# Delta rule and attention of a hybrid transformer layer: the strict mask first and its row factor on VectorE, turned k and q earlier, high parts on ScalarE and GpSimd, other places for early tiles

## The chip, the cores and the metric

One core of one Trainium2 chip runs the whole layer in one launch. The metric is the device time of that launch in microseconds. A core has TensorE (PE in the rows; PEld is its weight load), VectorE (DVE), ScalarE (ACT), GpSimd (POOL) and SyncE (SP, which here only issues DMAs). The engines run their own queues in order and meet only at semaphores.

## What is computed

One layer on 2048 tokens of width 1024, float32. Cut to what matters here:

```python
qkv = silu(causal_dwconv(q, k, v)); q, k = l2_norm(q), l2_norm(k)      # 4 heads of 128
g = cumsum(log decay) in each chunk of 64; decay = exp(g_i - g_j) for j <= i
lower = where(j < i, (beta_i k_i . k_j) * decay, 0)      # strict: the mask "below"
attn  = where(j <= i, (q_i . k_j) * decay, 0)            # inclusive: the mask "upto"
u, w  = solve(I + lower, [v * beta, k * beta * exp(g)])
# scan over chunks: v_new = u - w S;  o = q exp(g) S + attn v_new;  S = exp(g_last) S + k_dec^T v_new
o_gdn = rms_norm(o) * silu(z)
o_mla = block-causal softmax attention, 4 heads, keys of 128 + 64 rotary columns
x = layer_norm(ALPHA x + [o_gdn, o_mla] w_out); then a SwiGLU feed-forward, a second norm,
x + sigmoid(x w_ple_gate) * (p w_ple)
```

## The kernel before

The program runs eight stages one behind the other, with a barrier of all engines between them: in-projection (tile names begin with in_), latents (lat_), delta rule (dr_), attention (at_), output projection (op_), feed-forward in (ff_), feed-forward out (fd_) and the gated embedding (em_). Outside the delta rule, products are made from split operands: a float32 is cut into a high part in fp32r and a low part (value minus high part), and three matmuls (hi*lo, lo*hi, hi*hi) stand for one.

**Delta rule** (`delta_rule`). 16 tiles of 128 tokens (two chunks), all four heads at a time as [128, 4, 128]. The order is written out by hand. `steps()` gives 19 rounds; in round r tile m=r is begun ("first"), tile e=r-1 has its 16x16 diagonal blocks inverted ("base"), tile n=r-2 is solved ("solve"), and tile t=r-3 advances the state ("advance"). Each engine has its own list of calls per round, in order:

- TensorE: `a_ws(t,0)`, `s_z(n,0)`, `a_out(t-1)`, `a_kv(t,0)`, `p_turn(m)` (transposes k into b1 and q into b0, L1096), `a_ws(t,1)` (L1180), `a_o(t,0)`, `s_y(n,0)`, `a_kv(t,1)`, `p_turn_v(m)`, `s_z(n,1)`, `a_o(t,1)`, `s_y(n,1)`, `p_gram_k(m)` (k.k into b0, L1132), `s_wu(n)`, `p_gram_q(m)` (q.k into b3, L1138, which raises `gram_done`).
- VectorE: `a_v(t,0)` (L1471), `s_z(n,0)`, `a_s(t,0)` (the state, four scalar_tensor_tensor, L1480), `a_v(t,1)`, `a_gate`, `s_u(n,0)`, `a_s(t,1)`, `p_kdec`, `p_newton`, `p_factors` (makes `made`, among it L's row factor), `p_kbg`, `s_z(n,1)`, `s_u(n,1)`, `p_lower(m)` (L = b0 * dec[:, 0], L1434), `p_attention(m)` (L1439), `spread(e)` (L1449), `a_norm(t)`.
- GpSimd: `sums(m)` (L1031), `substitute(e)` (29 small operations, L1039, L1047, L1049), `decayed(m)` (qdT, L1064), `masks(m)`: decay times `upto` (L1054), decay times `below` (L1056), and that times L's row factor (L1059).
- SyncE stores L to DRAM once `L_done` is raised, waits for the store, and reads the diagonal blocks of it back as `blk` for `substitute`.

`p_turn(m)` waits for `L_done` of the tile before (b0 must have been read). `spread(e)` gives `U`, for which `s_z(n,0)` of the next round waits.

**Attention** (`attention`). 32 blocks (4 heads, 8 query blocks of 256 rows in the order 7,0,6,1,5,2,4,3), 144 steps of one pair of key tiles each. Per step TensorE turns the probabilities of two steps ahead (L1702), multiplies values (L1716 to L1718) and makes score groups three blocks ahead (L1685 to L1689); VectorE makes the low part of the turned probabilities (`low`, L1814) and the maxima (L1782); ScalarE makes their high part (L1751) and the exponentials (L1738); GpSimd scales a block's probabilities (L1651). In steps 2 to 21 of each of the first three heads the next head's operands are split, 16 pieces of 128x512 read through a ring of 4 `raw` buffers: kind 0 is q, 1 is k, 2 is the rotary part of q (two copies), 3 is v. The high part is copied by VectorE (`split_highs`, L1825, L1826, L1828), the low part is made by GpSimd (L1659, L1662), and SyncE loads a buffer again once the low part of its last piece is done. Even heads use the tiles that stand in `at.parts` (made by `AttentionEarly`), odd heads tiles of the stage's own. TensorE waits for `const_sem` (the identity, made by GpSimd) before its first score.

**Places.** Most tiles are placed by an allocator, upwards. The classes derived from `Early` place theirs, counted down from the top of the usable SBUF, so that they can be loaded in the stage before: the even heads' operands, `kr` and `kr_hi`; `op_w_raw`, `ff_x_raw`, `ff_w_raw`; the split weights `fd_w_hi`, `fd_w_lo`, `em_w_hi`, `em_w_lo`. `top` is 229368 rounded down to a multiple of 32: 229344, which is 96 past a multiple of 128. So all of these begin 96 bytes past a multiple of 128.

## Time and profile before

| | us |
|---|---|
| median of 3 runs (lowest, highest) | 3357.72 (3351.21, 3359.09) |
| the profiled execution | 3339.58 |
| its span | 3338.0 |
| TensorE busy | 3081.1 (92%) |
| VectorE, ScalarE, GpSimd busy | 1648.7, 1056.6, 1057.2 |

The profiled execution is 18 us below the median of the others. By the names in the trace, the delta rule takes the time from about 663 to 1058 us, attention from 1061 to 1460, the output projection to 1669, feed-forward in to 2560, feed-forward out from 2568 to 3086, the embedding from 3096 to 3328. TensorE is the busy engine in all of them; where it is idle or at half clock, another engine or a DMA was waited for. A row's duration of a matmul is a modelled one that overlaps the next; counts in a stretch tell its pace.

### The profile page before, as it was taken

Reading aid. Unit: us, or ns where it says so; the run is one execution under the profiler, and the core shown is the slowest. Engines: PE = TensorE matmul, PEld = TensorE weight load, DVE = VectorE, ACT = ScalarE, POOL = GpSimd, SP = SyncE. Lnnn points to the kernel's source line nnn. Section 1 sums busy time; section 2 is a strip of 40 time slices with the busy share of each in tenths; the row PEclk is TensorE's granted clock in tenths of the full one; section 3 lists DMA queues with packets and bytes.
Section 4 is the critical chain, followed back from the end, with each engine's and each line's share of the span. In section 5 each row is a group of like instructions: output and inputs, shape, how many; then the busy total and the mean of one; then the engine's idle time right before and its main releaser. Section 6 shows DMA issues by size and latency. Waiting matters only on the chain. (4 is left out here: it accounts for less than half of the span.)

```text
span 3338.0 us, 44243 instructions
## 1 busy us (share of the span) xinstructions
PE 3081.1 (92%) x15074; PEld 2541.3 (76%) x15074; DVE 1648.7 (49%) x2773; ACT 1056.6 (32%) x2363; POOL 1057.2 (32%) x1184
## 2 busy tenths in 40 slices
PE   7999997869997889989979999899998999999898
PEld 5888885658886777878758888788887788887776
DVE  3654004536665777656585555865555433233433
ACT  2111014335554444542243333433333211111321
POOL 2322241066665555410073333543331000000122
PEclk9999998979998989999989999999999999999999
DMA  3211115422324211125723222232223433233433
GB/s 137 87 75 75 75 57 183 143 75 75 82 63 106 61 50 54 67 76 181 239 69 115 94 75 80 71 117 94 76 79 111 136 97 96 90 96 122 148 121 99
DMA packets 284412, 329.17 MB, mean 99 GB/s; under 512 B 33280, under 2 KB 224640, under 8 KB 279936
## 3 DMA queue, kind: packets, MB, share of 16 engines
q1 hardware_dynamic: 238632, 265.84, 25.0%
q0 software_dynamic: 12384, 45.09, 3.8%
q10 hardware_dynamic: 33280, 16.78, 1.8%
q8 instruction: 62, 1.02, 0.1%
q14 instruction: 54, 0.44, 0.0%
HBM read 210.73 MB, written 116.92 MB: 98 GB/s over the span
## 5 line engine op out<-in xcount | busy, mean ns | idle before, releaser
L2061 PE MATMUL ff_bank<-ff_x_hi,ff_w_lo 128*128 128x512 f32 x1240 | 488.3, 394 | 32.8 <-DVE ff_w_lo L2241 22.0
L2062 PE MATMUL ff_bank<-ff_x_lo,ff_w_hi 128*128 128x512 f32 x1240 | 487.4, 393 | 0.0
L2063 PE MATMUL ff_bank<-ff_x_hi,ff_w_hi 128*128 128x512 f32 x1240 | 486.9, 393 | 0.0
L2044 POOL TENSOR_TENSOR ff_w_sum<-ff_w_raw 128x512 f32<-128x512 f32 x210 | 299.6, 1436 | 496.9 <-DVE ff_w_lo L2241 438.0
L2061 PEld LDWEIGHTS ff_bank<-ff_x_hi,ff_w_lo 128*128 128x128 f32 x1240 | 235.7, 190 | 85.2 <-DVE ff_w_lo L2241 25.0
L296 PE MATMUL in_h_ps<-in_x_hi,in_w_lo 128*128 128x512 f32 x704 | 276.6, 393 | 25.0 <-POOL in_w_lo L252 25.0
L2451 PE MATMUL fd_acc<-fd_w_hi,fd_a_lo 128*128 128x512 f32 x704 | 280.1, 398 | 10.8 <-DVE fd_a_lo L2435 10.7
L2452 PE MATMUL fd_acc<-fd_w_lo,fd_a_hi 128*128 128x512 f32 x704 | 278.3, 395 | 0.0
L2453 PE MATMUL fd_acc<-fd_w_hi,fd_a_hi 128*128 128x512 f32 x704 | 278.1, 395 | 0.0
L297 PE MATMUL in_h_ps<-in_x_lo,in_w_hi 128*128 128x512 f32 x704 | 276.1, 392 | 0.0
L298 PE MATMUL in_h_ps<-in_x_hi,in_w_hi 128*128 128x512 f32 x704 | 276.0, 392 | 0.0
L2063 PEld LDWEIGHTS ff_bank<-ff_x_hi,ff_w_hi 128*128 128x128 f32 x1240 | 235.8, 190 | 49.7
L2062 PEld LDWEIGHTS ff_bank<-ff_x_lo,ff_w_hi 128*128 128x128 f32 x1240 | 235.8, 190 | 49.0
L2140 ACT ACTIVATE ff_w_hi<-ff_w_sum 128x512 fp32r<-128x512 f32 x210 | 132.5, 631 | 288.3 <-PE ff_bank L2063 267.1
L2435 DVE TENSOR_TENSOR fd_a_lo<-fd_a_raw,fd_a_hi 128x256 fp32r<-128x256 f32 x176 | 74.5, 423 | 286.2 <-ACT fd_a_hi L2425 286.2
L2425 ACT ACTIVATE fd_a_hi<-fd_a_raw 128x256 fp32r<-128x256 f32 x176 | 73.4, 417 | 361.4 <-PE fd_acc L2453 356.5
L1651 POOL TENSOR_TENSOR at_prob<-at_prob,at_scale 128x1536 f32<-128x1536 f32 (+4 forms) x112 | 137.8, 1261 | 149.3 <-DVE at_scale L1808 141.1
L296 PEld LDWEIGHTS in_h_ps<-in_x_hi,in_w_lo 128*128 128x128 f32 x704 | 133.4, 189 | 53.8 <-issue 16.8
L2530 POOL DMA_DIRECT2D scratch_x<-fd_w_raw x16 | 8.5, 534 | 511.8 <-DVE fd_w_raw L2631 511.8
L2451 PEld LDWEIGHTS fd_acc<-fd_w_hi,fd_a_lo 128*128 128x128 f32 x704 | 132.2, 188 | 45.1 <-DVE fd_w_lo L2432 10.8
L2453 PEld LDWEIGHTS fd_acc<-fd_w_hi,fd_a_hi 128*128 128x128 f32 x704 | 132.2, 188 | 32.7
L2452 PEld LDWEIGHTS fd_acc<-fd_w_lo,fd_a_hi 128*128 128x128 f32 x704 | 132.3, 188 | 31.4
(380 smaller groups left out, 6582.6 us busy)
## 6 DMA issues: line engine op xcount, KB each, us to landing
ff_w_raw<-w_gate_up SPq DMA_DIRECT2D x44, 1024.0 KB, 5.1
scratch_hT<-in_out SPq DMA_DIRECT2D x22, 1024.0 KB, 3.9
fd_a_raw<-scratch_hid SPq DMA_DIRECT2D x176, 128.0 KB, 2.1
dr_qkv<-scratch_hT SPq DMA_DIRECT2D x16, 768.0 KB, 5.1
in_w_raw<-w_in POOLq DMA_DIRECT2D x22, 512.0 KB, 3.9
scratch_hid<-ff_first SPq DMA_DIRECT2D x44, 256.0 KB, 2.3
scratch_hid<-ff_second SPq DMA_DIRECT2D x44, 256.0 KB, 2.3
fd_w_raw<-w_down SPq DMA_DIRECT2D x22, 512.0 KB, 5.3
```

What stands on the lines that cost most here:

```text
L296: pe.matmul(acc, w_lo[:, b, ws], x_hi[:, k, ts], start=(k == 0), stop=False)
L297: pe.matmul(acc, w_hi[:, b, ws], x_lo[:, k, ts], start=False, stop=False)
L298: last = pe.matmul(acc, w_hi[:, b, ws], x_hi[:, k, ts], start=False, stop=(k == KD - 1))
L1651: last = pool.tensor_tensor(view, view, by, ALU.mult)
L2044: pool.tensor_tensor(w_sum[:, SUM_SLOT[m]], w_raw[:, b, one], w_raw[:, b, two], op).then_inc(w_sum_done, 1)
L2061: pe.matmul(acc, w_lo[:, wm, ws], x_hi[:, xm, k], start=first_mm, stop=False, skip_group_check=skip)
L2062: pe.matmul(acc, w_hi[:, wm, ws], x_lo[:, xm, k], start=False, stop=False, skip_group_check=skip)
L2063: return pe.matmul(acc, w_hi[:, wm, ws], x_hi[:, xm, k], start=False, stop=last_mm, skip_group_check=skip)
L2140: act.activation(w_hi[:, m], src, ACT.Copy).then_inc(w_hi_done, 1)
L2451: pe.matmul(to, self.a_lo[:, slot, rows], self.w_hi[:, k, cols], start=(k == k0), stop=False)
L2452: pe.matmul(to, self.a_hi[:, slot, rows], self.w_lo[:, k, cols], start=False, stop=False)
L2453: last = pe.matmul(to, self.a_hi[:, slot, rows], self.w_hi[:, k, cols], start=False, stop=(k == k1))
```

## The change

Six things, in three parts of the program.

In the delta rule: (1) GpSimd runs `masks(m)` ahead of `decayed(m)`, with `below` first, then `upto`; the third operation (row factor, L1059) is gone, so `masked` counts 2 a tile. (2) VectorE's `p_lower` applies the row factor: four scalar_tensor_tensor, one a head, in place of one tensor_tensor; it waits for the first mask alone, and `p_attention` for the second. (3) TensorE runs `p_turn(m)` straight after `a_ws(t, 0)`.

In attention: (4) VectorE's `split_highs` is gone. ScalarE copies the high parts of q and of the rotary part, and GpSimd makes those of k and v by adding a zero that is broadcast from a [128, 1] tile, ahead of the low part. (5) TensorE waits for the identity at its first transpose and no longer before its first score.

Places: (6) `top` is rounded down to a multiple of 128 (229248), so that every early tile begins at a multiple of 128. Of the tiles that TensorE reads with them: `fd_a_hi` and `fd_a_lo` begin 32 past a multiple of 128 before and now, `em_a_hi`, `em_a_lo` and the odd heads' operands at 0. The new `zero` tile moves those placed after it in attention by 32 bytes: `prob` from 0 to 32, `pT_hi` and `pT_lo` from 64 to 96.

```diff
@@ class Early
-        top = self.nc.sbuf_usable_end // 32 * 32
+        top = self.nc.sbuf_usable_end // P * P
@@ delta_rule, GpSimd
             def masks(m):
                 pool.wait_ge(dec_done, m + 1)
+                reached(pool, L_done, m)
+                pool.tensor_tensor(dec[:, 0], dif[:, m % 2], each(below[:]), ALU.mult).then_inc(masked, 1)
                 reached(pool, attn_done, m)
                 pool.tensor_tensor(dec[:, 1], dif[:, m % 2], each(upto[:]), ALU.mult).then_inc(masked, 1)
-                reached(pool, L_done, m)
-                pool.tensor_tensor(dec[:, 0], dif[:, m % 2], each(below[:]), ALU.mult).then_inc(masked, 1)
-                pool.wait_ge(masked, 3 * m + 2)
-                pool.wait_ge(made_done, 3 * (m + 1))
-                pool.tensor_tensor(dec[:, 0], dec[:, 0], heads(made[:, m % 2, 2]), ALU.mult).then_inc(masked, 1)
...
                 if m is not None:
+                    masks(m)
                     decayed(m)
-                    masks(m)
@@ delta_rule, TensorE
                 if advance:
                     a_ws(t, 0)
+                if first:
+                    p_turn(m)
                 if solve:
                     s_z(n, 0)
...
                     a_kv(t, 0)
-                if first:
-                    p_turn(m)
@@ delta_rule, VectorE
-                reached(dve, masked, 3 * (m - 1))
...
             def p_lower(m):
                 dve.wait_ge(gram_done, m + 1)
-                dve.wait_ge(masked, 3 * m + 3)
+                dve.wait_ge(masked, 2 * m + 1)
...
-                dve.tensor_tensor(L[:, m % 3], b0[:], dec[:, 0], ALU.mult).then_inc(L_done, 1)
+                for h in range(HEADS):
+                    op = dve.scalar_tensor_tensor(L[:, m % 3, h], b0[:, h], made[:, m % 2, 2, h:h + 1], dec[:, 0, h],
+                                                  ALU.mult, ALU.mult)
+                op.then_inc(L_done, 1)
...
             def p_attention(m):
                 dve.wait_ge(gram_done, m + 1)
+                dve.wait_ge(masked, 2 * m + 2)
@@ attention, GpSimd
             def low(h, m):
-                pool.wait_ge(split_high, count + 1)
+                if kind % 2 == 0:
+                    pool.wait_ge(act_high, count // 2 + 1)
+                else:
+                    if h > 1 and m == 1:
+                        pool.wait_ge(pv_done, pair0[NB * (h - 1)])
+                    pool.wait_ge(raw_loaded[slot], sum(32 if j % 4 == 2 else 16 for j in range(slot, count + 1, RAW)))
+                    high = (k_hi if kind == 1 else v_hi)[b]
+                    pool.tensor_tensor(high[:, ts], src, zero[:, 0:1].broadcast_to([P, NTOK]), ALU.add).then_inc(pool_high, 1)
+                    pool.wait_ge(pool_high, count // 2 + 1)
...
+            pool.memset(zero[:], 0.0).then_inc(const_sem, 1)
@@ attention, TensorE
             def turn(n, p):
+                if k == 0:
+                    pe.wait_ge(const_sem, 3)
...
-            pe.wait_ge(const_sem, 2)
@@ attention, ScalarE
+            def split_high(h, m):
+                count, slot, kind, ts = piece(h, m)
+                b, src = h % 2, raw[:, slot]
+                if h > 1 and m == 0:
+                    act.wait_ge(pv_done, pair0[NB * (h - 1)])
+                act.wait_ge(raw_loaded[slot], sum(32 if j % 4 == 2 else 16 for j in range(slot, count + 1, RAW)))
+                if kind == 2:
+                    reached(act, split_low, count + 1 - 4)
+                    act.activation(qr_hi[:], src, ACT.Copy)
+                    act.activation(qr[b][ROPE:, ts], src[ROPE:], ACT.Copy).then_inc(act_high, 1)
+                else:
+                    act.activation(q_hi[b][:, ts], src, ACT.Copy).then_inc(act_high, 1)
...
                 for group in now:
                     exps(*group)
+                for h, m in pieces:
+                    if m % 2 == 0:
+                        split_high(h, m)
@@ attention, VectorE
-                for h, m in pieces:
-                    split_highs(h, m)
```

How the rows of two queues stand. GpSimd in a round of the delta rule, from the end of a substitution (`dr_inv`) to the start of the next; before:

```order
L1049 TENSOR_TENSOR dr_inv<-dr_inv,dr_part 32x14
L1064 TENSOR_TENSOR dr_qdT<-dr_qkv,dr_eg 128x512
L1054 TENSOR_TENSOR dr_dec<-dr_dif,dr_upto 128x512
L1056 TENSOR_TENSOR dr_dec<-dr_dif,dr_below 128x512
L1059 TENSOR_TENSOR dr_dec<-dr_dec,dr_made 128x512
L1031 TENSOR_TENSOR dr_cums<-dr_upto,dr_scal 128x512
L1039 TENSOR_TENSOR dr_inv<-dr_ident_b,dr_blk 32x256
```

and of the change:

```order
L1049 TENSOR_TENSOR dr_inv<-dr_inv,dr_part 32x14
L1054 TENSOR_TENSOR dr_dec<-dr_dif,dr_below 128x512
L1056 TENSOR_TENSOR dr_dec<-dr_dif,dr_upto 128x512
L1061 TENSOR_TENSOR dr_qdT<-dr_qkv,dr_eg 128x512
L1031 TENSOR_TENSOR dr_cums<-dr_upto,dr_scal 128x512
L1039 TENSOR_TENSOR dr_inv<-dr_ident_b,dr_blk 32x256
```

Between the substitution and what `p_lower` waits for stood four operations; now there is one.

TensorE from one round's last product (q.k) to the next round's `a_ws(t, 1)`; before:

```order
L1138 MATMUL dr_b<-dr_qkv 128x128 x4
L1180 MATMUL dr_b<-dr_S,dr_wT 64x128 x4
L1151 MATMUL dr_b<-dr_ident,dr_U 128x128 x2
L1153 MATMUL dr_b<-dr_U,dr_L 128x128 x2
L1151 MATMUL dr_b<-dr_ident,dr_U 128x128 x2
L1153 MATMUL dr_b<-dr_U,dr_L 128x128 x2
L1096 MATMUL dr_b<-dr_ident,dr_on 128x128 x4
L1187 MATMUL dr_b<-dr_vnew,dr_kdec 128x128 x4
L1096 MATMUL dr_b<-dr_ident,dr_qkv 128x128 x8
```

and of the change:

```order
L1135 MATMUL dr_b<-dr_qkv 128x128 x4
L1177 MATMUL dr_b<-dr_S,dr_wT 64x128 x4
L1093 MATMUL dr_b<-dr_ident,dr_qkv 128x128 x8
L1148 MATMUL dr_b<-dr_ident,dr_U 128x128 x2
L1150 MATMUL dr_b<-dr_U,dr_L 128x128 x2
L1148 MATMUL dr_b<-dr_ident,dr_U 128x128 x2
L1150 MATMUL dr_b<-dr_U,dr_L 128x128 x2
L1093 MATMUL dr_b<-dr_ident,dr_on 128x128 x4
L1184 MATMUL dr_b<-dr_vnew,dr_kdec 128x128 x4
```

The eight transposes of k and q (`dr_qkv` x8) stood last of these, ahead of the product that waits for the new state; now they stand ahead of the products that wait for `U`. GpSimd in attention, the first four pieces of the second head, of the change:

```order
L1671 TENSOR_TENSOR at_q_lo<-at_raw,at_q_hi 128x512
L1665 TENSOR_TENSOR at_k_hi<-at_raw,at_zero 128x512
L1671 TENSOR_TENSOR at_k_lo<-at_raw,at_k_hi 128x512
L1668 TENSOR_TENSOR at_qr<-at_raw,at_qr_hi 64x512
L1665 TENSOR_TENSOR at_v_hi<-at_raw,at_zero 128x512
```

Before, only the four low parts stood there; each add of `at_zero` is a high part that VectorE made. That makes 24 operations more for GpSimd, 36 more for ScalarE (L1778, L1779, L1781) and 60 fewer for VectorE in the whole stage.

## Rows read from the trace of the kernel before

**Rows 1.** The page, part 1: busy time and instructions of each engine.
```profile
PE 3081.1 (92%) x15074; PEld 2541.3 (76%) x15074; DVE 1648.7 (49%) x2773; ACT 1056.6 (32%) x2363; POOL 1057.2 (32%) x1184
```

**Rows 2.** Timeline, one round of the delta rule: start us, us, engine, line, tiles [idle before].
```profile
853.18 1.06 PE L1138 MATMUL dr_b<-dr_qkv 128*128 128x128 f32 x8
853.27 1.04 POOL L1059 TENSOR_TENSOR dr_dec<-dr_dec,dr_made 128x512 f32<-128x512 f32 x1
854.40 0.69 DVE L1434 TENSOR_TENSOR dr_L<-dr_b,dr_dec 128x512 f32<-128x512 f32 x1 [3.28 <-POOL dr_dec L1059]
...
856.35 0.44 PE L1151 MATMUL dr_b<-dr_ident,dr_U 128*128 128x128 f32 x2 [1.09 <-DVE dr_U L1449]
...
859.48 1.09 PE L1096 MATMUL dr_b<-dr_ident,dr_qkv 128*128 128x128 f32 x8
859.59 1.12 DVE L1480 SCALAR_TENSOR_TENSOR dr_S<-dr_S,dr_eg,dr_b 128x128 f32<-128x128 f32 x4 [0.58 <-PE dr_b L1187]
859.90 0.85 POOL L1039 TENSOR_TENSOR dr_inv<-dr_ident_b,dr_blk 32x256 f32<-32x256 f32 x1 [4.58 <-DMA dr_blk<-scratch_blocks_L]
...
860.77 0.76 PE L1180 MATMUL dr_b<-dr_S,dr_wT 128*64 128x128 f32 x5 [0.19 <-DVE dr_S L1480]
```

**Rows 3.** Timeline, VectorE's L1434 in rounds 0 and 1; GpSimd after the first substitution.
```profile
684.43 0.69 DVE L1434 TENSOR_TENSOR dr_L<-dr_b,dr_dec 128x512 f32<-128x512 f32 x1 [3.40 <-POOL dr_dec L1059]
700.21 1.25 POOL L1064 TENSOR_TENSOR dr_qdT<-dr_qkv,dr_eg 128x512 f32<-128x512 f32 x1
705.12 0.69 DVE L1434 TENSOR_TENSOR dr_L<-dr_b,dr_dec 128x512 f32<-128x512 f32 x1 [15.17 <-POOL dr_dec L1059]
```

**Rows 4.** Timeline: VectorE's L1434, rounds 3 and 15; the latest of GpSimd's third masks.
```profile
749.71 0.69 DVE L1434 TENSOR_TENSOR dr_L<-dr_b,dr_dec 128x512 f32<-128x512 f32 x1 [3.15 <-PE dr_b L1138]
979.11 1.06 PE L1138 MATMUL dr_b<-dr_qkv 128*128 128x128 f32 x8
979.94 1.04 POOL L1059 TENSOR_TENSOR dr_dec<-dr_dec,dr_made 128x512 f32<-128x512 f32 x1
1001.81 0.69 DVE L1434 TENSOR_TENSOR dr_L<-dr_b,dr_dec 128x512 f32<-128x512 f32 x1 [3.25 <-POOL dr_dec L1059]
```

**Rows 5.** Windows in attention: busy of each engine (x instructions), clock, DMA share, GB/s.
```profile
1099.00:1149.00 50.00, 42.79 (x250) 37.47 (x248) 38.25 (x78) 21.88 (x60) 29.39 (x25) 0.90 0.23 67
1180.00:1252.00 72.00, 61.27 (x361) 53.60 (x360) 55.13 (x103) 30.59 (x82) 40.09 (x32) 0.88 0.19 56
1284.00:1355.00 71.00, 59.67 (x362) 52.55 (x361) 55.38 (x104) 30.10 (x81) 40.75 (x32) 0.90 0.18 54
1386.00:1443.00 57.00, 53.70 (x364) 47.93 (x363) 34.01 (x84) 29.57 (x82) 21.37 (x18) 1.00 0.25 91
1402.00:1443.00 41.00, 38.87 (x256) 34.45 (x255) 24.45 (x62) 21.34 (x61) 14.99 (x14) 1.00 0.33 122
```

**Rows 6.** Timeline, start of the second head: GpSimd's scaling; two of VectorE's copies.
```profile
1188.85 6.74 POOL L1651 TENSOR_TENSOR at_prob<-at_prob,at_scale 128x1536 f32<-128x1536 f32 x4 [12.13 <-DVE at_scale L1808]
1193.11 2.02 DVE L1828 CAST at_k_hi<-at_raw 128x512 fp32r<-128x512 f32 x1
1203.79 0.42 DVE L1828 CAST at_q_hi<-at_raw 128x512 fp32r<-128x512 f32 x1
```

**Rows 7.** Groups by line and form: same operations on ScalarE (delta rule's end) and GpSimd.
```profile
L1343 ACT ACTIVATE at_q_hi<-dr_qkv 128x512 fp32r<-128x512 f32 x2 | 1.2, 614 | 0.0
L1651 POOL TENSOR_TENSOR at_prob<-at_prob,at_scale 128x512 f32<-128x512 f32 x32 | 33.6, 1056 | 33.8 <-DVE at_scale L1808 33.8
```

**Rows 8.** Windows, TensorE alone, one of each stage: in, op, fd, em (columns as rows 5).
```profile
150.00:250.00 100.00, 100.00 (x443) 1.00 0.20 78
1494.00:1612.00 118.00, 118.00 (x563) 1.00 0.61 199
2633.00:2950.00 317.00, 317.00 (x1402) 1.00 0.31 96
3200.00:3300.00 100.00, 100.00 (x426) 1.00 0.39 120
```

21 lines of the change are left out of this document (5 added, 16 removed).

## The prediction

> **What bounds the kernel now.** The page first: TensorE is busy for 92% of the span, the others for half or less [rows 1], so a part of the change is worth only the time that TensorE waits, or runs at half clock, for what the part touches. I then read the timeline of one round of the delta rule, the windows of attention with and without split pieces, and the number of matmuls that equal stretches of the split products hold.
>
> In the delta rule two loops of nearly the same length close in `p_lower`. One is GpSimd's: L (L1434) starts at 854.40, its store and read back let the substitution start at 859.90, four mask operations follow it, and the next L comes 20.8 us after the last. The other is VectorE's and TensorE's: the q.k product ends at 854.24 (853.18 + 1.06), GpSimd's third mask operation at 854.31, so only 0.07 us lies between them; from L on, VectorE's queue (L, attn, U, the norm, v_new) and TensorE's lead to the state at 860.71 (859.59 + 1.12) and to L1180 at 860.77 [rows 2]. TensorE idles 1.09 and 0.19 us in this round, and from 860.77 to the next q.k product it has work throughout. So freeing GpSimd uncovers the second loop at once, except in the first rounds, where nothing is advanced yet: L of round 1 waits 15.17 us, all of it for GpSimd [rows 3].
>
> In attention the first five blocks of a head take 72 us in the second head and 71 in the third (1180:1252, 1284:1355), with split pieces in them, and 57 in the last (1386:1443), which has the same matmuls (361, 362 and 364 records) and no pieces. The granted clock is 0.88 and 0.90 against 1.00, and VectorE is busy for 77% against 60% [rows 5]. That pair is the experiment on which the largest term rests.
>
> **The change part by part.**
>
> *Masks, start-up.* Round 0: `below` takes the place of `upto`, L starts two operations earlier: 684.43 less 1.26 and 1.08 (with gap), so 2.3 earlier. L itself gets longer: four scalar_tensor_tensor took 1.12 for the state against 0.69 for the one tensor_tensor [rows 2], 0.43 more, so it is done 1.9 earlier. Round 1: the substitution starts 1.9 earlier, and between its end at 700.2 and L at 705.12 stand qdT (1.25), upto (1.22), below (1.22) and the product (1.1) [rows 3]; only `below` stays, 3.6 less. L starts 5.5 and is done 5.1 earlier. Round 2 gives the same again: L 8.7 earlier. Round 3 is bound by `U` (read back from DRAM after the substitution), some 7.4 earlier, and TensorE's eight transposes no longer lie in its path (0.6 of them showed). So round 3's L comes 8 us earlier than 749.71 [rows 4].
>
> *Masks, steady rounds.* From 749.71 to 1001.81 there are 12 rounds, 21.01 us each [rows 4]. GpSimd's third mask ended 0.07 after the q.k product in the round shown [rows 2] and 0.81 after it in the latest of the 12 (980.98 against 980.17) [rows 4]; the mean over them is 0.31, and that goes. L takes 0.43 longer in the second loop. Net +0.1 x 12 = +1. Moving `p_turn` costs and gives nothing: its 1.09 us fill the wait for `U` (1.09, then about 0.4), and the place that they leave, between 859.48 and 860.77, becomes a wait of about 1.2 for the state, since L1180 follows the state and not the transposes. Behind the new wait for L's reading of b0 stand `s_z` and `a_kv`, but L is done 1.2 after the q.k product and `a_ws` and the k half need 1.6. The third GpSimd operation (16 x 1.04) is hidden both ways. The delta rule: -8 + 1 = **-7** (bounds -11, if the steady rounds lose their idle too, and +6, if start-up gives nothing and 13 rounds pay 0.43).
>
> *High parts.* All of it gone would be worth 72 - 57 = 15, 71 - 57 = 14, and in the first head 50 - 41 = 9 (1099:1149 against 1402:1443, the same four blocks) [rows 5]: 38 us. Most of it is not the copying: a free copy takes 0.42, one beside GpSimd's scaling of 6.74 us took 2.02 [rows 6]; the 60 copies are 57 us of VectorE. ScalarE now has 36 copies at 0.61 [rows 7], 22 us, at 42% busy where VectorE stood at 77 [rows 5]. If each us there cost what it cost on VectorE (38/57), 15 would come back; if it is covered, none. I take 10, nearer the first, since these copies stand ahead of the next step's high part. GpSimd gets 24 adds with a broadcast operand, 1.06 each [rows 7], 8.5 us a head; it was busy 40 of 72 us. With the adds it needs 49 of about 60, and its results are wanted some steps later, so this is covered. If the cover fails, ScalarE waits for a `raw` buffer (a rival below). VectorE's small products with two SBUF operands can still meet GpSimd; that is in the 10. Attention: 38 - 10 = **-28** (bounds -38 and -10).
>
> On these copies the rows and a rule differ. The Trainium skill (GPSIMD Engine Reference, Engine selection) says to keep elementwise work on VectorE, as GpSimd takes about twice as long. The rows agree on the durations, 1.06 against 0.42; by the rule the k and v copies would come out 24 x 0.64 = 15 us worse. But TensorE does not wait for the sum of both engines' times, and the 2.02 in the rows is a copy that VectorE had to wait for.
>
> *The identity.* Scores start without it; the wait for it was a tail of under 1 us behind the stage's barrier, which stays: **-0.5** (bounds -1 and 0).
>
> *Places.* 100 us of TensorE at full clock hold 443 matmuls of 512 columns in the in-projection and 426 in the embedding [rows 8]: 0.226 and 0.235 each. In the output projection (118 us, 563 with some 80 transposes of 0.11) it is 0.226, in feed-forward out (317 us, 1402 with 80 transposes) 0.233. What goes with it, by the places in the program: moving and stationary operand begin at the same distance past a multiple of 128 bytes in the fast ones (0 and 0; 32 and 32), at different ones in the slow (96 and 32; 96 and 0). The embedding becomes 0 and 0: 960 x 0.009 = 8.6, of which I take 6, as part of it may be waits of the stage's own. Feed-forward out becomes 0 and 32, still unlike: I take 0 for its 2112 matmuls (bounds: -15 if it falls to 0.226, +4 if it goes to 0.235). The scores of the odd heads become all 0: -2.5; `prob` and `pT` become unlike the identity and v: +1. Places: **-7.5** (bounds -25 and +5).
>
> The Trainium skill (SBUF — State Buffer, two separate sides) has TensorE's port waiting for nobody, and its rule on operand starts speaks of legality alone. By it this part gives 0. No row shows a cause; the rows show the two paces.
>
> **Sum.** -7 - 28 - 0.5 - 7.5 = -43 against the profiled 3339.6, so 3296.6 there. The median of the runs lies 18 above the profiled one; the same difference puts it at 3357.7 - 43 = **3314.7**.
>
> **Rivals.** (a) *Places give nothing*: 3357.7 - 35.5 = 3322. For it: no row ties pace to place. Against: four stages in two kinds. (b) *ScalarE takes VectorE's place* in the chain turned, high, low, values: attention gives its lower bound of 10, 3357.7 - 25 = 3333. For it: every high part of the turned probabilities goes through ScalarE. Against: 42% busy. (c) *Feed-forward out gets faster too*, -14: 3301. (d) *Slower*: GpSimd becomes the bound in attention. ScalarE's copy of piece m waits for the buffer that GpSimd frees with the low part of piece m - 4, and that stands behind a scaling; with ScalarE waits everything. If each scaling in a head's first five blocks held it (6.7 [rows 6] and four smaller, 22 us in all), three heads would cost 66: 3357.7 - 43 + 66 = 3381. It decides once ScalarE reaches a piece before GpSimd is done with the fourth piece before it; I expect that once a head, for about 1 us. (e) *The change does not do what it says*: GpSimd's shorter row of masks never shows, because the second loop binds even the first rounds: +6 in place of -7, so 3328.
>
> **How the numbers follow.** Forecast 0.50; (a) 0.14; (b) 0.13; (c) 0.12; (d) 0.04; (e) 0.02; and 0.05 that several of (a), (b) and (e) together leave under 10 us of gain. The range runs from 3298, just under (c), to 3338, just over (b); it leaves out what is left of (d) and of the last case, and gains over 60. A measurement of this kernel tells 0.3% (10 us) from no change: faster 0.91, same 0.05, slower 0.04.
>
> **What would show it.** Round 3's L near 742 in place of 750, and rounds of 21.1 us after it, with VectorE's L released by the q.k product. TensorE idle about 0.4 before the turned `U` and 1.2 before the product that reads the new state. The blocks of the second head near 60 us, clock near 1.00, no 2 us copies. 100 us of the embedding with 440 matmuls or more, feed-forward out with its 1402 in 317 us unchanged. Wrong: steady rounds well under 20.8, ScalarE waiting for `raw`, TensorE waiting for GpSimd's low parts at a head's start, or the embedding still at 426.

## The result, and the profile after

The changed kernel took 3325.8 us (median of 7 executions, 3321.2 to 3337.8) beside 3351.2 for the kernel before on the same chip (7, 3343.4 to 3359.1). The ratio is 0.9935, with a 95% interval of 0.992 to 0.9951: 16 to 27 us gained. The profiled execution took 3321.2 us with a span of 3319.7, 18.3 less than the 3338.0 of before. I had forecast 43 less and 3314.7 in all. The sign and the range held, but only about half of the forecast gain came: 25 us between the medians, 22 by the ratio, 18 between the two profiled executions. The time itself looks nearer than that, 11 us off, because the kernel before came out at 3351.2 over seven executions and not at the 3357.7 of three from which I had counted; that is luck. By stage, from the first TensorE instruction of each stage to that of the next, worked out from the two traces:

| stage | before | after | difference | forecast |
|---|---|---|---|---|
| delta rule | 395.8 | 397.7 | +1.9 | -7 |
| attention | 406.4 | 391.7 | -14.7 | -30 (copies, identity, places) |
| feed-forward out | 527.4 | 528.5 | +1.1 | 0 |
| embedding | 241.9 | 238.7 | -3.2 | -6 |
| the four others | 1749.7 | 1746.2 | -3.5 | 0 |

The last row is scatter: the output projection, whose code did not change, lies between 206.7 and 210.5 in the fourteen traces of this study. Stages with the same code differ by up to 4 us elsewhere too (feed-forward out 527.4 to 530.9), the delta rule by much more, as will be seen. "Half clock" below means that the granted clock of TensorE is at its lower level, 1.2 GHz in place of 2.4. The first part of the page, which answers to [rows 1]:

```profile
PE 3070.0 (92%) x15074; PEld 2537.1 (76%) x15074; DVE 1598.8 (48%) x2761; ACT 1075.1 (32%) x2399; POOL 1060.7 (32%) x1193
```

**Delta rule.** The timeline of the changed kernel, VectorE, in the first four rounds (start us, us, engine, line, tiles, idle before). It answers to [rows 3, 4].

```profile
683.57 1.13 DVE L1431 SCALAR_TENSOR_TENSOR dr_L<-dr_b,dr_made,dr_dec 128x128 f32<-128x128 f32 x4 [2.15 <-POOL dr_dec L1054]
701.14 1.13 DVE L1431 SCALAR_TENSOR_TENSOR dr_L<-dr_b,dr_made,dr_dec 128x128 f32<-128x128 f32 x4 [12.08 <-POOL dr_dec L1054]
705.64 0.69 DVE L1449 TENSOR_TENSOR dr_U<-dr_u_blk,dr_diag 128x512 f32<-128x512 f32 x1 [2.58 <-DMA dr_u_blk<-scratch_blocks_U]
720.66 1.13 DVE L1431 SCALAR_TENSOR_TENSOR dr_L<-dr_b,dr_made,dr_dec 128x128 f32<-128x128 f32 x4 [3.78 <-POOL dr_dec L1054]
...
746.38 1.12 DVE L1431 SCALAR_TENSOR_TENSOR dr_L<-dr_b,dr_made,dr_dec 128x128 f32<-128x128 f32 x4 [3.15 <-PE dr_b L1135]
```

The stage begins 1.8 us later than before (667.8 us against 666.0), so round 3's L is 5.1 us earlier relative to it, and not 8. What is missing lies between L and the substitution. SP's queue in round 1, the changed kernel first, then the kernel before:

```profile
701.32 0.38 SPq L977 DMA_DIRECT2D dr_u_blk<-scratch_blocks_U  x1
702.29 0.45 SPq L980 DMA_DIRECT2D scratch_blocks_L<-dr_L  x1
706.13 1.39 SPq L987 DMA_DIRECT2D dr_blk<-scratch_blocks_L  x4
```

```profile
701.75 0.38 SPq L977 DMA_DIRECT2D dr_u_blk<-scratch_blocks_U  x1
705.84 0.33 SPq L980 DMA_DIRECT2D scratch_blocks_L<-dr_L  x1
707.89 1.39 SPq L987 DMA_DIRECT2D dr_blk<-scratch_blocks_L  x4
```

L is stored earlier, and now goes out 1.0 us behind the load of U's blocks. The read back is issued 3.84 us after the store in place of 2.05, and U itself is late (VectorE waits 2.58 us for it). From the end of L to the start of the substitution it is 6.6 us in place of 4.8, in round 1.

A steady round of the changed kernel, and in it TensorE's wait for the new state, which answers to [rows 2]:

```profile
875.14 1.06 PE L1135 MATMUL dr_b<-dr_qkv 128*128 128x128 f32 x8
876.24 1.13 DVE L1431 SCALAR_TENSOR_TENSOR dr_L<-dr_b,dr_made,dr_dec 128x128 f32<-128x128 f32 x4 [3.15 <-PE dr_b L1135]
884.33 0.76 PE L1177 MATMUL dr_b<-dr_S,dr_wT 128*64 128x128 f32 x5 [1.22 <-DVE dr_S L1480]
```

L follows the q.k product by 0.04 us in every round from the fourth on, an undisturbed round takes 21.08 us and the wait for the state is 1.22, all as forecast. But four of the twelve rounds take 22.4 to 22.7. In one of them `U` is late (TensorE waits 1.66 us for it); in the other three the clock falls to half for 3.4 us behind the wait for the state. Two windows of 4 us behind that wait, one with such a fall and one without, TensorE alone (window, length, busy (x instructions), granted clock, DMA share, GB/s):

```profile
839.27:843.27 4.00, 4.00 (x24) 0.57 0.29 79
883.93:887.93 4.00, 3.60 (x32) 1.00 0.02 6
```

In the first the granted clock is at 1.2 GHz for most of the time, and the round is 1.6 us longer. The trace of the kernel before has no such fall in its steady rounds; its waits for the state are 0.19 us and those for `U` 0.96 to 1.83.

**The identity.** TensorE's gap before its first score was 5.33 us, ended by the identity; now it is 4.66, ended by its own queue. The 0.7 us gained, 0.5 forecast, lie in the delta rule's row of the table, since that stage is counted to attention's first TensorE instruction.

**Attention.** Windows of the changed kernel over the same blocks as [rows 5] (busy of TensorE, its weight loads, VectorE, ScalarE, GpSimd; clock; DMA):

```profile
1180.00:1246.00 66.00, 58.02 (x360) 51.23 (x359) 34.44 (x83) 37.47 (x96) 45.53 (x39) 0.92 0.22 61
1278.00:1344.00 66.00, 56.38 (x357) 49.45 (x356) 35.12 (x84) 36.99 (x93) 46.68 (x40) 0.93 0.20 59
1375.00:1432.00 57.00, 53.76 (x364) 48.20 (x363) 34.11 (x84) 29.60 (x82) 21.38 (x18) 1.00 0.25 91
```

The five blocks take 66 us in place of 72 and 71, and I had said near 60, at a clock near 1.00; it is 0.92 and 0.93. VectorE's load fell as it should (55 to 34 us), and with it the copies of 2 us: 21 of the 60 copies of before took over 1 us. The longest waits left stand at one place of each head, the third and fourth block (GpSimd, SyncE's queue, ScalarE, TensorE):

```profile
1211.20 5.53 POOL L1652 TENSOR_TENSOR at_prob<-at_prob,at_scale 128x1024 f32<-128x1024 f32 x4 [3.30 <-DVE at_scale L1836]
...
1216.69 1.28 POOL L1668 TENSOR_TENSOR at_qr<-at_raw,at_qr_hi 64x512 fp32r<-64x512 f32 x1
1217.94 1.03 POOL L1665 TENSOR_TENSOR at_v_hi<-at_raw,at_zero 128x512 fp32r<-128x512 f32 x1
1218.00 1.09 SPq L1869 DMA_DIRECT2D at_raw<-scratch_qrT  x2
1219.05 1.28 POOL L1671 TENSOR_TENSOR at_v_lo<-at_raw,at_v_hi 128x512 fp32r<-128x512 f32 x1
...
1221.51 0.63 ACT L1778 ACTIVATE at_qr_hi<-at_raw 128x512 fp32r<-128x512 f32 x1 [1.53 <-DMA at_raw<-scratch_qrT]
...
1224.50 0.47 ACT L1749 ACTIVATE at_prob<-at_score_ps,at_negm 128x256 f32<-128x256 f32 x1 [1.20 <-DVE at_negm L1810]
...
1225.11 0.33 PE L1695 MATMUL at_score_ps<-at_k_hi,at_q_lo 128*128 128x128 f32 x1 [1.81 <-ACT at_prob L1749]
```

ScalarE waits 1.53 us for a piece that is still being loaded. Its load went out at 1218.00, when GpSimd had done the low part that frees the buffer (1216.69 + 1.28), and that stood behind a scaling of 5.53 us. The exps come late, TensorE waits 1.81 and then 1.45 us, and the granted clock is at half from 1225.5 to 1235.7. The other two heads show the same (ScalarE waits 1.43 and 1.55 us for the load). Two of the prediction's signs of being wrong are there: this one, and TensorE waiting for GpSimd's low part of v at the start of two heads, 0.6 us each.

**Places.** Windows of the changed kernel, feed-forward out and embedding, all engines (columns as above); they answer to the last two of [rows 8].

```profile
2617.00:2934.00 317.00, 317.00 (x1403) 256.26 (x1402) 101.15 (x210) 58.84 (x130) 5.31 (x10) 1.00 0.31 95
3185.00:3285.00 100.00, 99.78 (x432) 80.07 (x430) 38.08 (x43) 21.32 (x43) 26.72 (x22) 1.00 0.38 119
```

Feed-forward out keeps its pace (1402 matmuls before). The embedding goes from 426 to 432. Most of its matmuls of 512 columns now follow one another at 0.226 or 0.227 us; before they did at 0.231 or 0.238. By their pace it would be about 440, but TensorE's weight loads also wait for VectorE's low part of the activations. They did before, just as often; now each wait is longer. Who waited for that low part, in 200 us of the stage, before and after (us, times):

```profile
  PEld em_gate_ps L2451: 4.7, 14
```

```profile
  PEld em_gate_ps L2464: 6.6, 14
```

One of these in the changed kernel (GpSimd and VectorE):

```profile
3184.83 2.38 POOL L2696 TENSOR_TENSOR em_y<-em_y,em_xt 128x1024 f32<-128x1024 f32 x1 [9.59 <-DVE em_y L2742]
...
3185.33 2.17 DVE L2448 TENSOR_TENSOR em_a_lo<-em_a_raw,em_a_hi 128x256 fp32r<-128x256 f32 x1 [0.58 <-ACT em_a_hi L2438]
```

VectorE's low part takes 0.42 us by itself. Begun while GpSimd adds, it takes 2.17 and ends about 0.3 after GpSimd does. In the trace of before the longest takes 2.18.

### The profile page after: what moved, and what is told of

It reads as the page before. It is cut to its first block and busy times, and to the rows that moved or that the text cites. A ratio compares the mean times of both kernels' runs of the same rounds, so it can differ in the third digit from the quotient of the medians.

```text
span 3319.7 us, 44267 instructions
## 1 busy us (share of the span) xinstructions
PE 3070.0 (92%) x15074; PEld 2537.1 (76%) x15074; DVE 1598.8 (48%) x2761; ACT 1075.1 (32%) x2399; POOL 1060.7 (32%) x1193
## 5 line engine op out<-in xcount | busy, mean ns | idle before, releaser
L2074 PE MATMUL ff_bank<-ff_x_hi,ff_w_lo 128*128 128x512 f32 x1240 | 487.5, 393 | 32.3 <-DVE ff_w_lo L2254 16.2
```

The costliest lines, as they stand in the source:

```text
L2074: pe.matmul(acc, w_lo[:, wm, ws], x_hi[:, xm, k], start=first_mm, stop=False, skip_group_check=skip)
```

## The experiments

Twelve kernels, each timed in five rounds with the kernel before beside it. A ratio is that of a kernel to the kernel before in its own rounds; a stage's time comes from the one profiled execution. "Twelve rounds" is the time from the q.k product of round 3 to that of round 15.

**One part at a time.** The edits are the three parts of the diff: the delta rule, attention, and the line on the places.

> Before, with the delta-rule part of the change alone (GpSimd's order of masks, the row factor on VectorE, the turned k and q first). In the changed kernel the stage (its first TensorE instruction to the next stage's) took 397.7 us against 395.8, and four of its steady rounds had a stretch of 3.4 us at half clock behind TensorE's wait of 1.22 us. Theory A, the loss is the change's own: the stage is again 1 to 3 us longer than 395.8, rounds of 21.08 us with some of 22.5, and the kernel's ratio to before is 0.999 to 1.002. Rival, the slower stage came with the places (the early tiles' new starts) or by chance: the stage is 389 to 391 us here and the ratio near 0.998.

Measured: ratio 1.0007 (0.999 to 1.0025). The part alone gains nothing over twelve executions, though its start-up gain is there (4.7 us in its profile), so the loss is its own and not the places'. In the profiled execution the delta rule took 411.6 us, with 30.7 us at half clock in the twelve rounds, more than either theory had it; undisturbed rounds are again 21.08. 20.5 of the 30.7 are one fall that began while TensorE waited for a `U` whose blocks came late:

```profile
812.84 0.69 PE L1148 MATMUL dr_b<-dr_ident,dr_U 128*128 128x128 f32 x2 [3.29 <-DVE dr_U L1449]
```

Its twelve executions spread from 3338.8 us (mean clock 0.964) to 3369.6 (0.957).

> Before, with the attention part alone (high parts on ScalarE and GpSimd, the wait for the identity moved). Attention took 406.4 us in the kernel before and 391.7 in the changed one. If the copies alone are the cause, the stage is 391 to 393 here and all other stages are as before: ratio 0.995 to 0.997. Rival, part of the 14.7 came from the places of the odd heads' operands: then 394 to 396 here. prob and pT start 32 bytes later here as in the changed kernel, so a loss by that would be in this number.

Measured: ratio 0.9952 (0.9939 to 0.9965), attention 393.7. Nearly all of attention's gain is the copies'. Its delta rule is that of the kernel before, and this time had a fall of 3.4 us in the twelve rounds (255.5 us; the stage 398.5).

> Before, with the one line on the places alone. By the residue theory (a pass of 512 columns takes 0.226 us where moving and stationary operand start at the same distance past a multiple of 128 bytes and about 0.233 where they don't): the embedding's spacing goes from 0.231 and 0.238 to 0.227 and the stage from 241.9 to 238 to 239; feed-forward out keeps 527 to 529; attention gets 0 to 3 us shorter through the odd heads; in all -3 to -6 us, ratio 0.998 to 0.999. Rival, places give nothing and the embedding's gain in the changed kernel had another cause: the stage stays at 241.9.

Measured: ratio 0.9983 (0.997 to 0.9996); embedding 237.8, feed-forward out 528.9, attention 406.7. The embedding is as the residue theory has it, and the odd heads gained nothing. Its delta rule, again that of the kernel before, took 405.6 us, with 17.1 at half clock in the twelve rounds: such falls come without the change too. The three parts' ratios multiply to 0.9942, which agrees with the 0.9935 of the whole.

**The place of the transposes.** The edit moves `p_turn(m)` from behind `a_ws(t, 0)` back to behind `a_kv(t, 0)`.

> The changed kernel with p_turn back behind a_kv(t, 0), where it was before. Theory: in the changed kernel the transposes no longer fill the time in which the product that reads the new state waits, the wait is 1.22 us in one piece, and behind four of 13 such waits the clock fell for 3.4 us, 1.6 us lost each; put back, the waits before the turned U and before that product are about 1.1 to 1.5 and 0.2, no half clock lies in the steady rounds, all of them take 21.0 to 21.1 us and the delta rule's stage is 391 to 393 us against 397.7. Rival, the half clock comes by the phase of the rounds whatever the order of the work: as many stretches as in the changed kernel and 396 to 398 us. Second rival, the transposes in the old place hold round 3's start-up up by 0.6 us each: then the gain is 2 us smaller.

Measured: ratio 0.9936 (0.9921 to 0.9952), the delta rule 395.0, twelve rounds 253.4 us with no half clock, each 21.08 to 21.34. The rounds are as the theory has them; the stage is 2 us above its range, since round 3's product comes 1.4 us later than in the changed kernel, as the second rival has it. But the median is that of the changed kernel. One profile is also not enough here, because the falls differ between executions of the same kernel; I took it up again at the end. TensorE's two waits of a round are these:

```profile
876.09 0.44 PE L1148 MATMUL dr_b<-dr_ident,dr_U 128*128 128x128 f32 x2 [1.40 <-DVE dr_U L1449]
880.51 0.76 PE L1177 MATMUL dr_b<-dr_S,dr_wT 128*64 128x128 f32 x5 [0.19 <-DVE dr_S L1480]
```

In the changed kernel they are 0.38 and 1.22. The same 1.6 us stands in two pieces in both orders, and the longest piece is longer here, where no fall came.

**Starts of the tiles.** In the changed kernel, with 96 bytes of padding ahead of feed-forward out's activation tiles and attention's tiles reordered (the edit, cut to the tiles that matter):

```
+        if s.stage == "fd":
+            s.sb("pad", [P, 24])
         self.a_hi = s.sb("a_hi", [P, 2, 2 * P], F32R)
...
-        zero = s.sb("zero", [P, 1])
         prob = [s.sb(f"prob{n}", [P, 2, (SEQ, SEQ // 2)[n % 2]]) for n in range(4)]
+        pT_hi = s.sb("pT_hi", [P, T_RING, 2 * QB], F32R)
+        pT_lo = s.sb("pT_lo", [P, T_RING, 2 * QB], F32R)
         negm = s.sb("negm", [P, 4, 2, 4])
...
-        pT_hi = s.sb("pT_hi", [P, T_RING, 2 * QB], F32R)
-        pT_lo = s.sb("pT_lo", [P, T_RING, 2 * QB], F32R)
+        zero = s.sb("zero", [P, 1])
```

> The changed kernel with 96 bytes of padding ahead of feed-forward out's activation tiles, so that they start at a multiple of 128 bytes as its weights now do, and with attention's small tiles behind prob and pT, so that all its operands start at such a multiple. Residue theory: feed-forward out's passes of 512 columns go from 0.231 to 0.238 us to 0.227, its stage from 528.5 to 512 to 516 us; attention gets 0 to 4 us shorter; the kernel 13 to 18 us faster than the changed one (ratio to before near 0.989). Rival, the start of a tile is not what sets the pace there (the embedding got faster by other means): the stage keeps 528 and the ratio stays at 0.9935.

Measured: ratio 0.9905 (0.9886 to 0.9924). Feed-forward out took 516.7 us in place of 528.5, and its window shows why:

```profile
2618.00:2935.00 317.00, 317.00 (x1444) 1.00 0.31 96
```

1444 matmuls stand where 1403 stood, with nothing else done to this stage than its activation tiles and what follows them moved by 96 bytes. Attention stayed at 393.2, where its time with these copies is 391.6 to 393.7 in all other traces but those of the last two versions: the starts of `prob` and `pT` make no difference that shows there.

**Six buffers for the pieces**, `RAW = 6` in place of 4.

> The changed kernel with six buffers for the pieces in attention in place of four. In the changed kernel ScalarE waits once a head, 1.5 us, for a piece's load, whose buffer GpSimd frees late, behind a scaling; the exps come late, TensorE waits 1.8 and 1.4 us and then runs at half clock for 7 to 10 us. Theory, this wait gives most of what attention did not gain: ScalarE's wait for the load goes, the third and fourth block of a head take 25 us in place of 28, attention 382 to 386 against 391.7. Rival, ScalarE's copies and exps themselves are the cause and the load is hidden behind them: 390 to 393.

Measured: attention 391.6 (the ratio, 0.9947, holds a delta rule of 405.0). The rival's number came. The mechanism is another than either had: ScalarE no longer waits for the load, and TensorE waits 3.75 us at the same place all the same:

```profile
1232.99 1.28 POOL L1671 TENSOR_TENSOR at_k_lo<-at_raw,at_k_hi 128x512 fp32r<-128x512 f32 x1
1233.34 0.94 DVE L1820 TENSOR_TENSOR at_gap<-at_top,at_negm 128x4 f32<-128x4 f32 x1
...
1236.58 1.26 POOL L1671 TENSOR_TENSOR at_v_lo<-at_raw,at_v_hi 128x512 fp32r<-128x512 f32 x1
1236.95 0.91 DVE L1836 TENSOR_TENSOR at_scale<-at_fac,at_total 128x4 f32<-128x4 f32 x1
1237.78 1.27 DVE L1810 TENSOR_REDUCE at_negm<-at_score_ps 128x1 f32<-128x512 f32 x2
1238.56 0.69 ACT L1749 ACTIVATE at_prob<-at_score_ps,at_negm 128x512 f32<-128x512 f32 x1 [3.27 <-DVE at_negm L1810]
1239.39 0.80 PE L1695 MATMUL at_score_ps<-at_k_hi,at_q_lo 128*128 128x512 f32 x1 [3.75 <-ACT at_prob L1749]
```

Two products of four columns take 0.94 and 0.91 us in place of 0.16, and each ends within 0.02 us of GpSimd's operation (1232.99 + 1.28 = 1234.27 and 1234.28; 1237.84 and 1237.86). The maximum that ScalarE needs stands behind them. In the changed kernel itself no such product took more than 0.59 us, so this second stall shows only where the load no longer comes first.

The Trainium skill (GPSIMD Engine Reference, Specifications) says that GpSimd shares its SBUF interfaces with VectorE and that VectorE's instructions with two SBUF inputs contend with it. The trace agrees: the products with two SBUF inputs end with GpSimd's operation, and the two maxima, which read PSUM, take 1.27 us for both, where one by itself takes 0.68.

**Without the high parts.** For heads 1 to 3 ScalarE's copies and GpSimd's adds are left out; a second run leaves out the adds alone. The operands of these heads are then zeros or those of an earlier head, and whether that changes the time by itself no run tells. The edit is cut to its main lines.

```
-                pool.tensor_tensor(high[:, ts], src, zero[:, 0:1].broadcast_to([P, NTOK]), ALU.add).then_inc(pool_high, 1)
...
-                    if m % 2 == 0:
-                        split_high(h, m)
```

> The changed kernel without the high parts of the pieces of heads 1 to 3 (the copies on ScalarE and the adds on GpSimd are left out; their tiles are zeroed once before). It sizes what they cost altogether. By the difference of the heads with and without pieces in the kernel before (38 us of 406.4), attention takes 370 to 374 us. Rival, part of that difference belongs to the low parts on GpSimd and to the loads, which stay: then 376 to 384.

Measured: attention 367.8, that is 38.6 us less than before the change and 2 below the lower end of what was expected. The second head's first blocks, 361 matmuls in 72 us before, stand in 57:

```profile
1171.00:1228.00 57.00, 53.96 (x373) 48.72 (x372) 33.20 (x80) 30.64 (x84) 35.35 (x27) 1.00 0.18 50
```

The 38 of the prediction are right, and what the new high parts cost is 391.7 - 367.8 = 23.9 us, where I had put 10.

> The changed kernel without GpSimd's 24 adds that make the high parts of k and v of heads 1 to 3 (left out; their tiles are zeroed once before); ScalarE's copies stay. All high parts together gave 23.9 us of attention (391.7 to 367.8). Theory, what attention did not gain is VectorE's small products of two SBUF operands waiting for GpSimd's operations, a run of which lasts some 8 us with the adds in it: without them attention takes 374 to 380. Rival, ScalarE's copies ahead of the high parts of the turned probabilities are the cause: 386 to 390.

Measured: attention 393.0 (ratio 0.9949). Both theories fall: leaving out the 24 adds alone gives nothing. ScalarE's wait for the load is still there (1.42 to 1.51 us a head), so this run does not show that the adds are free of cost in a kernel without that stall. It does show where they are not felt. In the whole stage TensorE waits as follows for the low part of the turned probabilities, which VectorE makes after ScalarE's high part (us in total, times, longest; the changed kernel, without the adds, without all high parts):

```profile
PE at_acc_ps L1728 <- DVE at_pT_lo L1842: 16.8, 20, 1.8
```

```profile
PE at_acc_ps L1728 <- DVE at_pT_lo L1842: 16.7, 20, 1.8
```

```profile
PE at_acc_ps L1725 <- DVE at_pT_lo L1836: 11.7, 19, 1.7
```

These waits do not change with GpSimd's adds; they shrink only when ScalarE's copies go as well.

**Maxima ahead of the small products**, on VectorE:

```
+                for group in now:
+                    maximum(*group)
                 if whole is not None:
                     scales(whole)
-                for group in now:
-                    maximum(*group)
```

> The changed kernel with one order turned round on VectorE: in each step of attention the maxima of the new scores ahead of the four small products of a block's scale. Nothing is left out. At a head's fourth block TensorE waits 1.8 and 1.4 us for ScalarE's exps, these for VectorE's maximum, and that stands behind the small products, each of which ends when a GpSimd operation ends. Theory: the two waits fall under 1 us, the half clock of 7 to 10 us behind them goes, the stage takes 381 to 386 against 391.7. Rival, the scaling on GpSimd then comes later and TensorE waits for the turned probabilities in its place: 390 to 394.

Measured: attention 392.6 (the ratio, 0.9958, and the profiled execution hold a delta rule of 423.8), as the rival has it, but again not by its mechanism. The waits of the changed order in the third and fourth block of a head (engine, line, waited for; us in total, times, longest):

```profile
PE at_score_ps L1695 <- ACT at_prob L1749: 3.7, 2, 2.4
...
ACT at_qr_hi L1778 <- DMA at_raw<-scratch_qrT: 2.1, 1, 2.1
```

Now ScalarE's wait for the load holds the exps, as in the changed kernel. Taking away either stall alone leaves TensorE waiting at this place for the other.

**The row factor on GpSimd, but first.** GpSimd's order is below, row factor, upto, qdT; L is one operation of 0.69 us again, and `p_turn` is late.

```
                 pool.tensor_tensor(dec[:, 0], dif[:, m % 2], each(below[:]), ALU.mult).then_inc(masked, 1)
+                pool.tensor_tensor(dec[:, 0], dec[:, 0], heads(made[:, m % 2, 2]), ALU.mult).then_inc(masked, 1)
                 pool.tensor_tensor(dec[:, 1], dif[:, m % 2], each(upto[:]), ALU.mult).then_inc(masked, 1)
```

> The changed kernel with the row factor back on GpSimd, but ahead of the other mask (below, factor, L; then upto, qdT), L as one operation of 0.69 us, and p_turn behind a_kv(t, 0). Theory: GpSimd's loop has 2.5 us of slack, the second loop is 0.43 shorter than in the changed kernel: steady rounds 20.65 us in place of 21.08, L still released by the q.k product; start-up 0.6 to 2 us longer than in the changed kernel; stage 388 to 391 us if no half clock lies in the rounds (397.7 in the changed kernel with four such stretches, 395.0 with p_turn late and none). Rival, GpSimd's factor product is late again and L waits for it: rounds of 20.9 to 21.1 and no gain.

Measured: ratio 0.9927 (0.9909 to 0.9946); undisturbed rounds 20.65 us, L 0.04 behind the q.k product in all of them, so the mechanism holds. The stage took 397.9 with 6.8 us of half clock in the twelve rounds and more around them, so its saving is not seen in this profile, and the ratio lies within the interval of `turn_late`'s.

**All together**: this order of masks, `p_turn` late, the padding, six buffers, and the maxima first.

> The changed kernel with five edits: GpSimd's row factor ahead of its other mask and p_turn late, feed-forward out's padding, six buffers for the pieces, and the maxima ahead of the small products. From the runs so far: delta rule 390 to 398 by the half clock in it, feed-forward out 517 (528.5 before), attention 380 to 390 if the order on VectorE and the buffers give what they should, 391 to 393 if neither does. Together 3300 to 3312 us beside a kernel before of 3347 (ratio 0.986 to 0.990); rival, the two edits of attention undo each other or give nothing: 0.990.

Measured: 3296.6 us beside 3347.1, ratio 0.9857 (0.9839 to 0.9876), the fastest of all and 3 us under what was expected. The delta rule took 388.4 (no half clock in its twelve rounds), feed-forward out 516.4, attention 380.0: the two edits of attention give nothing singly and 11.7 us together. Its second head's first five blocks, to be read beside the 66 us above:

```profile
1169.00:1230.00 61.00, 54.06 (x359) 47.75 (x358) 35.78 (x83) 36.93 (x95) 45.59 (x39) 1.00 0.22 66
```

The clock is at 1.00, TensorE's longest wait for exps there 1.18 us. The small products are still held as long as before (up to 0.95 us); what changed is that no maximum stands behind them.

**The place of the transposes again**, in this version: `p_turn` early.

> The version of the run combined with p_turn in the changed kernel's place (behind a_ws(t, 0)) and nothing else different. The seven profiled executions with p_turn there took 6 to 22 us more over the twelve steady rounds than twelve undisturbed rounds, always with stretches of half clock; the six with p_turn behind a_kv took 0 to 10 more (252.0 to 262.2 us for the kernel before's masks, 253.4, 254.6 and 251.0 for the others). Theory, the early place makes the clock fall: steady rounds of 20.65 broken by rounds of 22 and more, the twelve in 255 to 268 us against 251.0 in combined, kernel 4 to 15 us slower than combined (ratio to before 0.987 to 0.990). Rival, the place makes no difference and the half clock comes by chance: 250 to 254 us and a ratio within 0.001 of 0.9857.

Measured: 3305.3 us, ratio 0.9884 (0.9867 to 0.9901), by the ratios 9 us above the version with the late place, with intervals that just overlap. Attention took 378.5, so its gain came a second time. The delta rule took 398.2, the twelve rounds 255.0 in place of 251.0, and the round before them 31.2 in place of 25.5. The time is as the theory has it, but most of the stage's 9.8 us lie outside the steady rounds, and of the 4.0 in them about 3 are one round with a late `U` and a fall behind it. All fourteen traces together, twelve steady rounds:

| `p_turn` | us at half clock | sum of the waits for the state |
|---|---|---|
| behind `a_kv` (before, two of its parts, turn late, row factor first, combined) | 0, 17.1, 3.4, 0, 6.8, 0 | 2.3 in each |
| behind `a_ws` (after and seven others) | 10.2, 30.7, 6.8, 10.2, 13.7, 34.1, 34.1, 3.4 | 14.6 in each |

The mean is 4.6 us in the first row and 17.9 in the second. One trace of the late place has more than five of the early, so the place makes the falls likelier at most and does not decide them. The idle time is nearly the same in both: in the twelve rounds of the combined version all waits of TensorE add up to 17.1 us with `p_turn` late and 19.8 with it early.

What stood before the falls tells more. With the early place 22 of the 96 waits of 1.22 us for the state were followed by a fall within 0.6 us, 3.4 us long in all but one; three more falls, of 20.5 us each, began during waits of 3.3 to 3.5 us for a late `U`, and these three are 61 of the row's 143 us. Without them its mean is 10.2. With the late place none of the 72 waits of 0.19 us was followed by a fall: seven of its eight falls stood behind a wait for `U` of 1.8 to 2.6 us, the eighth behind one of 1.3 for another tile. Yet the twelve waits of 1.40 to 1.66 us for `U` in `turn_late` had none behind them. So how the idle time is divided does not explain the falls; the longer wait for the state goes with them. Why a wait of 1.22 us there is at times followed by half clock, and one of 1.40 us four microseconds earlier was not, no run here shows.

## Why the prediction was right and wrong

- **Start-up, -8**: the mechanism was right, the size 5. Every step of it was costed but the transfers: moving L earlier moved its store to just behind the load of U's blocks, and both came later. That the one delays the other is read from their order; no run moved the store alone. I had left the store and read back at their old duration ("the substitution starts 1.9 earlier", and the same again in round 2).
- **Steady rounds, +1**: undisturbed rounds are the 21.1 us of the forecast, released as forecast. The term that failed is "Moving `p_turn` costs and gives nothing". The wait of 1.22 us that it leaves before the product with the new state was forecast and priced at nothing; behind 22 of 96 such waits the clock fell, at about 1.6 us lost each. The twelve rounds took 252.0, 262.2 and 255.5 us in the three traces with the order of before, and 259.2 to 274.9 in the seven with the order of the change: about +9 on the mean and +7 in the pair of profiles. Of the seven, three have a round of 32.3 to 32.7 us behind a late `U`, which makes up about 5 us of their mean. That the part as a whole loses its start-up gain again is shown by its own run (ratio 1.0007). That `p_turn`'s place does it is likely and not shown: one pair of kernels that differ in it alone has the same median (0.9935 and 0.9936), the other is 9 us apart.
- **Rival (e)** was wrong in its mechanism, as the start-up gain came. Its time, 3328, and that of rival (a), 3322, lie nearer to the 3325.8 than mine, so the number alone could not have told them apart; the stages do.
- **The identity, -0.5**: 0.7.
- **High parts, -38**: 38.6 by the run that leaves them out. The pair of heads with and without pieces was a sound experiment.
- **Given back, +10**: 23.9, above even the 15 that I had as the most; this is the largest miss. It failed where I scaled the cost by ScalarE's busy time (22 us at 38/57) and left the wait for a `raw` buffer out of the sum. ScalarE's busy time did come as forecast; the cost lies in waits and in the clock behind them. The late load (the mechanism of rival (d), which I had as about 1 us once a head) and, once it is gone, VectorE's products held by GpSimd each stop the exps, TensorE waits 3.3 to 4.5 us a head for it, and 7 to 10 us at half clock follow. Both taken away together give 11.7 us, and the half clock in the stage falls from 36.7 to 14.7 us, against 12.8 without any high parts. The lower bound of 10 for attention (rival (b)) lies nearer to the 14.7 than my 28. The other 12 us (380.0 against 367.8) go in the main with a wait of rival (b)'s chain: in the combined version TensorE waits 20.1 us for the low parts of the turned probabilities, without high parts 11.7. No run left out ScalarE's copies alone, so this share is read from the waits and not shown by an experiment.
- **GpSimd's adds, covered**: right in the changed kernel, where taking them out gave nothing (393.0 against 391.7). TensorE does wait for GpSimd's low part of v behind them, but for 1.2 us in all. By the rule of the Trainium skill (GPSIMD Engine Reference, Engine selection), which keeps elementwise work on VectorE, they would have cost 15 us. The durations bear the rule out, by somewhat more than its factor of about two (1.04 us against 0.42), but hardly anybody waits for them here.
- **Places**: the paces went as the starts would have it. The embedding's -6 was right for the pace alone: the mean spacing fell from 0.2334 to 0.2271 us, 6.0 us over 960 matmuls. It became -3.2 because TensorE's waits for VectorE's low parts, there before, grew by 2 to 3 us in the stage; by the run with the places alone it is -4.1. The odd heads' -2.5 and the +1 for `pT` and `prob` did not show. Feed-forward out kept its pace, and rival (c) could be had for 96 bytes of padding: -11.8 us. By the Trainium skill (SBUF — State Buffer, two separate sides), where TensorE's port waits for nobody, places give 0; the runs of the padding and of the places alone show 11.8 and 4.1 us. What in the chip causes it, they do not show.
- **Rival (a)** is out by the run with the places alone; **(d)** as a slower kernel did not come, but its place was the right one.

## What to carry to other kernels

Where a queue feeds TensorE, look for every stall that ends at the same place before valuing one: here two edits gave nothing singly and 12 us together. For the same reason, leaving work out of a kernel that has another stall at that place does not show that the work is free. Take a tile's start into account when a stream of large matmuls runs slower than its neighbours, by counting matmuls in equal windows. And when work is moved out of a wait of TensorE's, do not put the wait that it leaves at nothing because the sum of the waits stays the same: look at the granted clock behind it, in more than one profile.

## What the runs showed of the hardware

- Matmuls of 512 columns follow one another at 0.226 to 0.227 us where the moving and the stationary operand start at the same distance past a multiple of 128 bytes, and at 0.231 to 0.238 where they do not. It held in two stages when only the start was changed (1403 to 1444 matmuls in 317 us; 426 to 432 in 100 us with waits). In both stages both operands then start at a multiple of 128; that an equal distance of 32 is as good rests on the one pair of that kind in the prediction, and no run tried it. In attention, with matmuls of 128, 256 and 512 columns and many waits, the starts made no difference that shows. Which part of the chip does this, no run shows.
- In the delta rule's steady rounds the granted clock fell to half behind 22 of 96 waits of TensorE of 1.22 us for the state, mostly for 3.4 us, and behind none of 72 waits of 0.19; three falls of 20.5 us began during waits of 3.3 to 3.5 us. Twelve waits of 1.40 to 1.66 us at another place of the round had no fall behind them.
- Executions of one kernel differ by 6 to 31 us, and the mean granted clock goes with it: 0.964 at 3338.8 us and 0.957 at 3369.6 for the same code.
- VectorE's operations with two SBUF inputs were held until GpSimd's ended: 0.94 us in place of 0.16 for a product of four columns, 2.17 in place of 0.42 for one of 256.
- A store and its read back that took 2.05 us from issue to issue took 3.84 when another load had been issued 1 us earlier.
